# Long convolution accumulated in PSUM, V pages of four samples side by side, and a later wait in the fox steps

## The reference

```
glu = c_v * sigmoid(c_g)
yc, conf_hist = causal_dwconv(glu, hist['conf'], p['conf_dw_w'])      # C: 31 taps, 512 channels
o_c = silu(layernorm(yc + p['conf_dw_b'], ...))

s = einsum('bqhd,bkhd->bhqk', qi, k) * (d ** -0.5)                     # D: forgetting attention, 8 heads of 64
s = s + swapaxes(ci, 1, 2)[..., None] - ck
p = softmax(where(k_pos <= q_pos, s, NEG_INF))
o = einsum('bhqk,bkhd->bqhd', p, v)
```

## Time and profile before

| | before |
|---|---|
| median of three runs | 1736.78 us (1733.03 to 1740.67) |
| the profiled execution | 1732.22 us |
| its span, first to last instruction | 1729.2 us |
| TensorE busy | 1486.3 us (86% of the span) |
| VectorE busy | 961.7 us (56%) |
| GpSimd busy | 563.1 us (33%) |
| ScalarE busy | 556.1 us (32%) |
| mean granted TensorE clock | 0.923 |

### The profile page before, as it was taken

The page is one execution under the profiler, slowest core; times in us unless marked ns, Lnnn a source line. Parts: engine busy times, 40 slices in busy tenths (PEclk is TensorE's granted clock), DMA queues, the critical chain, the costliest instruction groups (busy, mean ns, idle before and its releaser), DMA issues. The chain is left out here.

```text
span 1729.2 us, 28170 instructions
## 1 busy us (share of the span) xinstructions
PE 1486.3 (86%) x11055; PEld 1379.2 (80%) x11055; DVE 961.7 (56%) x1366; ACT 556.1 (32%) x858; POOL 563.1 (33%) x311
## 2 busy tenths in 40 slices
PE   5986878688887989789888879898669999999995
PEld 5886877688887989766666658898558999999995
DVE  3189896899968675533223332265246777772212
ACT  5322650212133222534222222355335223233222
POOL 3355453343442433011111103320504444443440
PEclk9988987899998999999888889999879999999997
DMA  7425432434442544258444436433323333332331
GB/s 201 130 68 145 118 115 68 131 90 116 123 128 86 147 116 129 68 164 256 125 134 134 128 103 201 130 86 103 127 69 104 89 95 95 90 98 71 101 92 50
DMA packets 254643, 199.83 MB, mean 116 GB/s; under 512 B 15780, under 2 KB 212957, under 8 KB 254104
## 3 DMA queue, kind: packets, MB, share of 16 engines
q1 hardware_dynamic: 234149, 169.47, 34.0%
q10 hardware_dynamic: 19371, 23.86, 4.2%
q0 software_dynamic: 992, 4.72, 0.8%
HBM read 187.89 MB, written 10.81 MB: 115 GB/s over the span
## 5 line engine op out<-in xcount | busy, mean ns | idle before, releaser
L836 PE MATMUL pb<-xh,wh 128*128 128x260 f32 x2176 | 642.0, 295 | 34.1 <-ACT ar L1195 16.6
L836 PE MATMUL pb<-xl,wh 128*128 128x260 f32 x2176 | 628.7, 289 | 0.0
L836 PE MATMUL pb<-xh,rawl 128*128 128x260 f32 x2176 | 627.1, 288 | 0.0
L790 POOL TENSOR_TENSOR rawl<-raw,wh 128x1024 fp32r<-128x1024 f32 (+2 forms) x152 | 343.9, 2263 | 859.1 <-ACT wh L1195 858.5
L836 PEld LDWEIGHTS pb<-xh,wh 128*128 128x128 f32 x2176 | 425.1, 195 | 42.0 <-issue 28.7
L836 PEld LDWEIGHTS pb<-xl,wh 128*128 128x128 f32 x2176 | 425.3, 195 | 0.5
L836 PEld LDWEIGHTS pb<-xh,rawl 128*128 128x128 f32 x2176 | 424.7, 195 | 0.0
L1195 ACT ACTIVATE wh<-raw 128x1024 fp32r<-128x1024 f32 (+2 forms) x208 | 201.6, 969 | 513.1 <-PE pb L836 463.3
L836 PE MATMUL sd<-ar 128*128 128x128 f32 (+7 forms) x1488 | 258.8, 390 | 95.9 <-DVE ar L1599 63.3
L836 PEld LDWEIGHTS sd<-ar 128*128 128x128 f32 (+4 forms) x1488 | 177.2, 192 | 141.5 <-issue 85.0
L805 POOL TENSOR_TENSOR ar<-ar 128x512 f32<-128x512 f32 x128 | 191.1, 1493 | 249.0 <-DMA ar<-in_cache_fox_k 226.7
(11 more groups left out here) (193 smaller groups left out, 1693.0 us busy)
## 6 DMA issues: line engine op xcount, KB each, us to landing
raw<-in_w_in SPq DMA_DIRECT2D x80, 512.0 KB, 4.2
ar<-in_cache_fox_k SPq DMA_DIRECT2D x128, 256.0 KB, 2.7
ar<-in_cache_fox_v SPq DMA_DIRECT2D x128, 256.0 KB, 3.1
raw<-in_w_ffn_in SPq DMA_DIRECT2D x44, 512.0 KB, 3.7
raw<-in_w_branch SPq DMA_DIRECT2D x32, 256.0 KB, 3.2
raw<-in_w_ffn_out SPq DMA_DIRECT2D x16, 512.0 KB, 3.9
ar<-in_cache_mem_k ACTq DMA_DIRECT2D x1, 4096.0 KB, 19.7
raw<-in_w_out SPq DMA_DIRECT2D x8, 512.0 KB, 3.9
```

The lines of the kernel that those rows point to most:

```text
L790: pool.tensor_tensor(rawl[:, p % RING, 0:kt, :], raw[:, p % RING, 0:kt, :], wh[:, p % (AHEAD + 1), 0:kt, :].bitcast(F32), SUB).then_inc(lo ...
L836: return pe.matmul(o, l, r, start=start, stop=stop, skip_group_check=True)
```

## The change

1. **Taps.** `TAPS` now runs through a block's 31 taps before the next block's. The accumulator of the block in work is the PSUM bank `s3`: the first tap writes it there, the next 29 read and write it there, and the last one reads it there and writes `oC` in SBUF. The samples' eight columns stay in `oC`. Each tap waits for the one before. As `s3` is taken, l2p uses banks 0 and 1 for the 512 prompt columns and some columns of bank 2 for the samples.
2. **Order.** Half of a slot's taps now stand before the pages of K, and half behind them.
3. **V pages.** The four pages of a group belong to four samples, one to a strip (`v_page`). A round is 16 groups, and there are two rounds; the heads' sums are made by strip (`own_strip` in place of the ones), four columns for each block, so masking, sums and copy run once for a round. `V_EVENTS` has 2 x (16 + 1) = 34 events.
4. **Fox steps.** From step 2 on TensorE waits at its start for VectorE's part of the step before only, and for its part of this step ahead of the value product.

```diff
--- before.py
+++ after.py
@@ -207,11 +207,17 @@
 
 
 MARKS = ("AFTER", "BEFORE", "TAPS", "REDUCES", "KSTART", "VSTART", "PAGES")
-TAPS = [(j, c) for pair in range(2) for j in range(CFW) for c in (2 * pair, 2 * pair + 1)]
+TAPS = [(j, c) for c in range(KB) for j in range(CFW)]
 N_TAP = len(TAPS)
 N_PAGE = PAGES * NB
-V_OF = PAGES // VG
-V_EVENTS = [x for b in range(NB) for x in [("v", V_OF * b + n) for n in range(V_OF)] + [("vx", b)]]
+V_EVENTS = [x for r in range(NB // VG) for x in [("v", PAGES * r + n) for n in range(PAGES)] + [("vx", r)]]
+
+
+def v_page(g, j):
+
+    return (VG * (g // PAGES) + j) * PAGES + g % PAGES
+
+
 
 
 def timeline():
@@ -332,8 +338,10 @@
                 out.append(("napply", 2, p - first_piece("kv")))
                 if p == last_piece("kv"):
                     out.append(("napply", 2, KD))
-            background("tap", {"cv": 4, "cg": 4, "gx": h, "ac": 2 - h, "ah": 2 - h, "ab": 2 - h}.get(kind, 2))
+            n_tap = {"cv": 4, "cg": 4, "gx": h, "ac": 2 - h, "ah": 2 - h, "ab": 2 - h}.get(kind, 2)
+            background("tap", n_tap - n_tap // 2)
             background("k", h if kind == "gx" else 1 + (p % 8 == 0))
+            background("tap", n_tap // 2)
     evac(NP_ - 1)
     through(("BEFORE", "END"))
     pos[0] = SIDE.index(("BEFORE", "END")) + 1
@@ -731,8 +739,9 @@
                 page("cache_fox_k", i, kring[:, i % 4, :], page_in[i % 4])
 
             def v_group(g):
-                for i in range(VG * g, VG * g + VG):
-                    page("cache_fox_v", i, v_slot(i), v_in[i % 8])
+                for j in range(VG):
+                    i = VG * g + j
+                    page("cache_fox_v", v_page(g, j), v_slot(i), v_in[i % 8])
 
             for p in range(2, RING - 1):
                 weights(p)
@@ -965,8 +974,9 @@
                 done = K if kind == "y" else K + 1
                 if upto(act_works, done):
                     pe.wait_ge(act_s.sem, upto(act_works, done))
-                if upto(dve_works, done):
-                    pe.wait_ge(dve_s.sem, upto(dve_works, done))
+                late = kind == "fox" and n >= 2
+                if upto(dve_works, K if late else done):
+                    pe.wait_ge(dve_s.sem, upto(dve_works, K if late else done))
                 if kind == "xr":
                     for j in range(2):
                         for t in range(QT):
@@ -1023,13 +1033,15 @@
                         for b in range((n - 1) % QT + 1):
                             last = tr(s1[:, b * P:(b + 1) * P], fP[:, b * P:(b + 1) * P])
                     if 2 <= n <= FOX + 1:
+                        pe.wait_ge(dve_s.sem, upto(dve_works, K + 1))
                         h, q = divmod(n - 2, QT)
                         for b in range(q + 1):
                             last = mm(s2[:, 0:P], vt[:, b, 192 * (h // 2) + FD * (h % 2):192 * (h // 2) + FD * (h % 2) + 2 * FD], fPT[:, b, :], b == 0, b == q)
                 elif kind == "l2p":
                     for j in range(2):
                         for h in range(2):
-                            last = mm(sd[:, 2 * j + h, 0:TH], ones, lsq2[:, j, h * TH:(h + 1) * TH])
+                            last = mm(sd[:, j, :], ones, lsq2[:, j, 0:SEQ]) if h == 0 else \
+                                mm(s2[:, NB * j:NB * j + NB], ones, lsq2[:, j, SEQ:T])
                 elif kind == "gp":
                     if n < 4:
                         for h in range(2):
@@ -1154,19 +1166,19 @@
 
                 if g == 0:
                     pe.wait_ge(dve_s.sem, upto(dve_works, ITEMS.index(("ds", 3)) + 1))
-                elif g % V_OF == 0:
-                    pe.wait_ge(v_out.sem, g // V_OF)
+                elif g % PAGES == 0:
+                    pe.wait_ge(v_out.sem, g // PAGES)
                 for j in range(VG):
                     i = VG * g + j
                     pe.wait_ge(v_in[i % 8], 16 * (i // 8 + 1))
-                    last = mm(s3[32 * j:32 * j + FH, :], sc[:, i, :], v_slot(i), g % V_OF == 0, g % V_OF == V_OF - 1)
+                    last = mm(s3[32 * j:32 * j + FH, :], sc[:, v_page(g, j), :], v_slot(i), g % PAGES == 0, g % PAGES == PAGES - 1)
                 v_used.by(last)
 
-            def v_heads(b):
-
-                pe.wait_ge(v_rows.sem, b + 1)
+            def v_heads(r):
+
+                pe.wait_ge(v_rows.sem, r + 1)
                 for c in range(KB):
-                    last = mm(s3[:, c:c + 1], vdiag[:, c * P:(c + 1) * P], ones[:, 0:1])
+                    last = mm(s3[:, VG * c:VG * c + VG], vdiag[:, c * P:(c + 1) * P], own_strip)
                 v_sum.by(last)
 
             for e in TIMELINE:
@@ -1391,7 +1403,8 @@
                         act.wait_ge(qs_out, 16)
                         act.dma_start(ssam[:, :, :], a["state_gdn"].rearrange("b l h k v -> k (b l h) v")).then_inc(ss_in, 16)
                     if n:
-                        fn(lrs2[:, :, :].rearrange("p j (h c) -> p (j h) c", h=2), sd[:, :, 0:TH], ACT.Ln, bias=eps6[:, 0:1])
+                        fn(lrs2[:, :, 0:SEQ], sd[:, 0:2, :], ACT.Ln, bias=eps6[:, 0:1])
+                        fn(lrs2[:, :, SEQ:T], s2[:, 0:2 * NB].rearrange("p (j b) -> p j b", j=2), ACT.Ln, bias=eps6[:, 0:1])
                         fn(lrs2[:, :, :], lrs2[:, :, :], ACT.Exp, a2v, scale=-0.5)
                     if n < 4:
                         act.wait_ge(ev_all.sem, count(dve_tile, mt_of("gx", 2 * n + 1)))
@@ -1716,16 +1729,21 @@
                 w = cols[:, B_CW, 0:124].rearrange("p (j c) -> p j c", c=KB)[:, :, c]
                 g = glu[:, c, :]
                 if j == 0:
-                    own(dve.tensor_scalar(oC[:, c, :], g[:, 30:30 + T], w[:, 30:31], col(V_CB + c), MUL, ADD))
+                    if c == 0:
+                        dve.wait_ge(pe_s.sem, upto(pe_works, ITEMS.index(("sm", 3))))
+                    else:
+                        dve.wait_ge(dve_c.sem, tap_at[c - 1])
+                    dve_c.by(dve.tensor_scalar(s3, g[:, 30:30 + SEQ], w[:, 30:31], col(V_CB + c), MUL, ADD))
+                    tap_at[c] = dve_c.n
+                    dve_c.by(dve.tensor_scalar(oC[:, c, SEQ:T], g[:, 30 + SEQ:30 + T], w[:, 30:31], col(V_CB + c), MUL, ADD))
                     hs = cols[:, B_CS:B_CS + NB, 0:120].rearrange("p b (j c) -> p b j c", c=KB)[:, :, :, c]
                     tt(htmp, hs, w[:, None, 0:30].to_broadcast([P, NB, 30]), MUL)
                     red(fl8, htmp, ADD)
                     tt(oC[:, c, SEQ:T], oC[:, c, SEQ:T], fl8, ADD)
                     return
-                if c in tap_at:
-                    dve.wait_ge(dve_c.sem, tap_at[c])
-                dve_c.by(dve.scalar_tensor_tensor(out=oC[:, c, 0:SEQ], in0=g[:, j - 1:j - 1 + SEQ], scalar=w[:, j - 1:j],
-                                                  in1=oC[:, c, 0:SEQ], op0=MUL, op1=ADD))
+                dve.wait_ge(dve_c.sem, tap_at[c])
+                dve_c.by(dve.scalar_tensor_tensor(out=oC[:, c, 0:SEQ] if j == CFW - 1 else s3, in0=g[:, j - 1:j - 1 + SEQ],
+                                                  scalar=w[:, j - 1:j], in1=s3, op0=MUL, op1=ADD))
                 tap_at[c] = dve_c.n
 
             def reduce_page(i):
@@ -2062,13 +2080,13 @@
                     reduce_page(e[1] - 1)
                 elif e[0] == "kend":
                     reduce_page(N_PAGE - 1)
-                elif e[0] == "v" and e[1] % V_OF == V_OF - 1:
+                elif e[0] == "v" and e[1] % PAGES == PAGES - 1:
                     dve.wait_ge(v_used.sem, e[1] + 1)
                     v_rows.by(dve.tensor_tensor(vdiag.rearrange("p (h d) -> p h d", h=FH), s3.rearrange("p (h d) -> p h d", h=FH),
                                                 spread(own_head, FD, 2), MUL))
                 elif e[0] == "vx":
                     dve.wait_ge(v_sum.sem, e[1] + 1)
-                    own(dve.tensor_copy(vo[:, :, e[1]], s3[:, 0:KB]), v_out)
+                    own(dve.tensor_copy(vo[:, :, VG * e[1]:VG * e[1] + VG], s3[:, 0:KB * VG].rearrange("p (c j) -> p c j", j=VG)), v_out)
 
 
 _INS = ["x_prompt", "x_sample", "cache_fox_k", "cache_fox_v", "cache_fox_logf", "cache_mem_k", "cache_mem_v",
```

## The result

The changed kernel takes 1685.7 us (median of four runs, 1678.3 to 1691.4) where the kernel before took 1737.0 on the same chip: a ratio of 0.9705, 95% interval 0.9681 to 0.9729. It is 51 us faster; the forecast was 68 us faster, 1669, with a range of 1640 to 1706. The profiled execution of after took 1689.8 us, its span 1688.0. A second set of four runs gave 1686.0 (ratio 0.9708, 0.9677 to 0.9738), and its profiled execution has a span of 1686.9.

What follows compares the result with a forecast made beforehand. VectorE was taken to pace 100 to 490 us, TensorE 803 to 996 us. Gains of 31 (taps) and 37 (fox steps) sum to 68 us: 1732.2 becomes 1664, plus 4.6 for the median, 1669; range 1640 to 1706.

Steps and rivals of the forecast that it cites:

- Taps in PSUM: 100 to 490 us: accumulator in PSUM ends GpSimd's hold-up; 120 taps take 82 us in place of 125.2, 43 less.
- slow bank: Taps: VectorE can't overlap reading and writing one PSUM bank; 1731 (no change) or 1760 (slower); chance 0.10, half each.
- it does not do what it says: Taps: GpSimd holds them through the SBUF input, so they stay at 125 us; 1702, chance 0.05.
- the chain: Taps waiting for their own result: 0.09 us for each of 16 exposed pairs, taken as 2 us; all exposed 11.
- Handed on: First stretch: GpSimd holds other VectorE operations instead; 10 us taken; as rival, three quarters of taps' gain, 1690, chance 0.20.
- What is left counts whole: 100 to 490 us: VectorE sets the pace, so its remaining 31 us (43 - 2 - 10) shorten the kernel fully.
- The fox steps: 803 to 996 us: fewer waits 15.6, clock 20 and later wait 1.6 make 37 us; bounds 25 to 45.
- the nine waits from 803 to 996 us: TensorE waits 20.0 us for VectorE's last fox product; seven of nine go with V pages side by side, 15.6 us.
- where I took 20: 803 to 996 us: TensorE's clock of 0.85 costs 29 us; 20 of it recovered when the waits go.
- The V groups that used to lie behind piece 96: Second stretch: about four more V groups, 1.04 us each, against four sums by head less (3.8 us).
- the later wait: Fox steps: logits start earlier, some 0.8 us at each of two waits left, 1.6 together; nothing at piece 96.
- that rival: Fox steps: V pages come late and TensorE waits for DMA; 12 us gained in place of 37, 1694; chance 0.13.

Runs made afterwards that it cites:

- e2: Kernel before with only the V pages of four samples side by side and what hangs on that: 1714.8 us, ratio 0.9879.
- e3: Kernel before with only the fox steps' later wait: 1721.7 us, ratio 0.9908.
- e4: Kernel before, V pages unmoved; VectorE only does a fox step before the V event (masking product or copy) directly ahead of it: 1692.5 us, ratio 0.9738.
- e1: Kernel before with only the taps in PSUM, block after block, and l2p's sums moved out of that bank: 1722.7 us, ratio 0.9916.
- e7: Changed kernel with every second middle tap left out (60 of 120): 1668.1 us, ratio 0.9605.
- e11: Kernel before with all of the change but the V pages, and VectorE's fox step ahead of the V event: 1669.0 us, ratio 0.9629.

## Why the forecast was right in kind, and 17 us too large

**Taps in PSUM: right, and a little dear.** No hold-up is left, and reading and writing one bank cost nothing: 754 ns against the undisturbed 750. So the slow bank (1731 or 1760) fell, and "it does not do what it says" (1702) too. By the Trainium skill, VectorE: DVE Perf Modes, section on the TRN2 errata, a tap from PSUM would be an estimated 65 ns longer; the runs show 4. The term that was mis-sized is the chain: I let 16 pairs pay it and put the tap at 0.68 us from start to start. In the rows all taps that follow a tap pay 0.10 us (3.12 and 3.10 against 2.73 for four), near the upper bound of 11 us that I gave and did not take. So 35.0 us less of taps, where I had 43 - 2 = 41. (The profile of before has the shortest taps: in e2, e3 and e4, with the same taps, they took 132.6, 127.8 and 130.0 us, so 35.0 is the low end.)

**Handed on: nothing, where I took 10.** VectorE's busy time from piece 10 to 50 fell from 351.8 to 308.5 us, 43.3 us (40.2 in the second profile): more than the taps' own 35. GpSimd's fell with it, in the same 106 instructions, from 183.8 to 172.4. So the two mistakes, a chain too cheap by 6 us and 10 us handed on that were not, go against each other: 31 forecast as VectorE's net loss, 40 to 43 had. VectorE's load fell by more than forecast, and the time by less.

**"What is left counts whole": the step that failed.** VectorE was busy 82 to 98% of the four stages of the earlier trace rows, and I read from that share that it paced all of them. It did so to piece 14: 15.8 us less busy, 14.9 us shorter. From 14 to 50 it lost 27.5 us and the stage 9.4 in one profile and 0.5 in the other, and of the 9.4 the clock has 7 (half rate for 65 us where before had 78.5); e1 shows the same, 27.9 against 0.8. Five profiles with this tap order give 343.9 to 352.8 us, 347.1 in the mean, against 353.3; but e4, with the taps of before, took 347.6, so those 6 us are not clear of what the stage varies by. So of the 31 us some 20 came at most (15 and 5). e7 shows the same stage from the other side: 25 us less of VectorE, 12 to 21 us shorter, more than half of it by the clock. TensorE's largest waits of that stage in after (141 to 485 us) are these:

```profile
PE sd L845 <- DVE ar L1612: 15.9, 12, 4.3
PE sd L845 <- ACT ar L1438: 14.6, 2, 8.3
```

They are small steps of VectorE and ScalarE in gdn's chains. Taps that get shorter move the first little (23.9 us in before and 18.5 in e4, 20.9 in e1, 15.9 and 19.1 in the two profiles of after; 9.1 with half the taps) and the second not at all (12.4 to 14.7 us in all six). An engine that is busy 86% of a stage (303.99 of 353 us) is not yet the one that ends last in it.

**The fox steps: mechanism right, parts mis-sized.** Forecast 37; pieces 82 to 98 give 30.1 and 35.6 us in the two profiles. Two masking products and two copies, and two waits in the body, came as forecast, at a clock of 0.96 and 0.97. But the nine waits from 803 to 996 us lay across two stages: six in the body, 14.7 us, and three already in the run at piece 96, where they are the steps' own chain and stayed. So the body gave 14.7 - 3.7 = 11.0 us of them and not 15.6, and 2.3 us of another wait. Its clock went from 0.87 over 160 us to 0.96 over 135, which is half rate for 41 and then 10 us: 15 us of cost gone where I took 20. The V groups that used to lie behind piece 96 came into it, three here where I said about four. By form of instruction, TensorE's V groups in the body of before:

```profile
L836 PE MATMUL sd<-ar 128*8 128x512 f32 x140 | 20.4, 619 | 0.0
```

and of after:

```profile
L845 PE MATMUL sd<-ar 128*8 128x512 f32 x164 | 25.3, 596 | 0.6 <-DMA ar<-in_cache_fox_v 0.5
```

That is 24 matmuls, 4.9 us more: 11.0 + 2.3 + 15.4 - 4.9 = 23.8 of the 24.8 us that the body lost. Against that, the later wait, which I counted at 1.6 us with nothing at piece 96, was worth more in this kernel: from e2, without it, to the two profiles of after, pieces 82 to 98 go from 217.1 to 209.5 and 204.0 us, and e3 alone gave 13. A single wait was mis-sized little: I took 0.8 us, where its own rows (869.98 - 869.02) give 0.96 and e3's waits 0.87. The V pages were hardly ever late (0.5 us of waits for their DMA in the body; 2.9 between pieces 62 and 82, where the kernel before has 2.0), so that rival fell.

**The clock elsewhere: not in the sum at all.** Stages that the change hardly touches got longer: 62 to 82 by 6.8 and 3.7 us, 130 to 140 by 3.5 and 2.5 us. In before and after the first of them has half rate for 13.7 and 23.9 us, which explains 5 of the 6.8; in the second profile it has 17.1 us, which explains 2 of the 3.7. e4, with none of the change in it, takes 190.4 us there with 20.5 us at half rate, so half of the 6.8 comes and goes without the change; and from 130 to 140 every profile but that of before takes 109 to 111 us, with or without it. The first is the clock's for the most part, and the some 2 us that remain are what the V pages alone cost there (e2); the second belongs to that one profile of before. Why the clock fell there stays open.

The account in the first profile: 14.9 + 9.4 + 24.8 + 5.3 us gained, 6.8 + 3.5 us given back there and 2 elsewhere, 42 us for the profiled pair; 51 between the medians. "Handed on" at 1690 lies nearest to the time among the rivals, and its mechanism is refuted: nothing was handed on, the gain was not on the path.

## What to carry to other kernels

A busy share says which engine is loaded, not which ends last: before a saving is counted whole, see in the same stage whether the idle time of the other engines ends with the loaded one, stage by stage, or leave half of the work out and look. Where an engine works a fixed list in order, look first at what stands ahead of the step that others wait for: moving an event behind it (e4, 42 us) was worth twice the restructuring that made the events fewer (e2, 20 us), and made it unnecessary (e11, 1669.0 us). An accumulator in PSUM freed VectorE from GpSimd here at no price per operation that could be seen (754 ns against 750), but a chain of operations on one accumulator cost 0.10 us for each.

## What the runs showed of the hardware that was not expected

VectorE reads and writes one PSUM bank in one operation as fast as SBUF: 741 to 757 ns over 116 taps, with GpSimd at work or not, against a median of 750 for all taps in SBUF. The hold-up had been mutual: from piece 10 to 14 the same 15 instructions of GpSimd took 27.87 us before and 24.54 after, from 14 to 50 the same 91 took 155.97 and 147.83 us. By the Trainium skill, SBUF — State Buffer, section "SBUF: two separate sides", the two engines share a pair of ports as an exclusive lock that VectorE takes with two SBUF inputs; these rows agree, on both sides of the lock.
